# The second weight block waits for x, and the memory's norm moves back by one to two ticks

## The chip, the cores and the metric

The kernel runs on one core of a Trainium2 chip. The core has four compute engines with a stream of instructions each: the matrix engine TensorE (PE in the rows, PEld for its weight loads), VectorE (DVE), ScalarE (ACT) and GpSimd (POOL). SyncE (SP) computes nothing here, it issues transfers. Each engine takes its own instructions strictly in order; between engines only semaphores order the work. The metric is the device time of one execution in microseconds (us).

## The reference

Two layers over 256 tokens of width 1024, batch 1, all in 32-bit floats. Each layer adds three things to x in turn: a mixing part, a cross-attention to 256 memory rows, and an expert part that gathers 16 of 16,384 experts for each of 8 heads. Cut to its core:

```python
for l in range(DEPTH):
    h = rmsnorm(x, norm_mix_g[l])
    p_conv, p_attn, p_ssm = split(h @ w_in[l])          # u, val, gate, q, k, v
    y_conv, y_attn, y_ssm = conformer_conv(p_conv), stick_breaking_attention(p_attn), s5_ssm(p_ssm)
    x = x + concat(rmsnorm(y_conv), rmsnorm(y_attn), rmsnorm(y_ssm)) @ w_out[l]
    x = x + memory_cross_attention(rmsnorm(x, norm_mem_g[l]), rmsnorm(mem, mem_norm_g[l]),
                                   w_mq[l], w_mkv[l], w_mo[l])
    x = x + peer_ffn(rmsnorm(x, norm_ffn_g[l]), peer_wq[l], peer_sub_keys[l], peer_u[l], peer_v[l])
return rmsnorm(x, final_norm_g)
```

The change concerns the first microseconds of layer 0: `h @ w_in` for the first 128 tokens, and `rmsnorm(mem, mem_norm_g[0])` with the first products of it, the memory's keys `mem_h @ w_mkv`.

## The kernel before

The 256 tokens are two chunks of 128, and with two layers there are four stages, numbered ci = 0 to 3. In each stage the chunk's normed rows are transposed to `hT` (8 tiles of 128 x 128), multiplied by weight blocks, and worked through convolution, state space model, attention, memory attention and expert queries. A weight block is 1 MB (1024 rows by 256 columns, as `[128, 2048]`). The blocks are named by what they make: u, val, gate, q (two), k (two), v (two), mk (four, the memory's keys), mv (four), and more. Each gives 16 matmuls of 128 x 128 per chunk, which the trace lists as 32 records. The expert part of a stage makes 128 gathers, each of which brings one expert's row of 8 KB for every token of the chunk (1 MB; 512 gathers in all, the first at about 178 us), while the next stage's blocks run between them.

The program is written by a schedule of ticks. Every engine has a list of generators ("strands"), one for each piece of work of a stage. A strand yields the tick at which its next piece is due; the writer of an engine goes through the ticks, and at each tick through the strands in the order of the list, and puts down all that is due. So the tick numbers and the list's order fix the order of instructions on each engine. They fix nothing between engines; that is done by semaphores alone.

Around the change stage 0 stands so:

- **SP** (`block.sync`) issues x (first 128 rows), the small parameters `prm` (68 KB), the gain rows, and then the blocks in the order in which PE takes them (`issue`, one number j for each). Some other transfers are put ahead of a certain j: the memory's rows (`memX`, 1 MB) ahead of j = 2, the parameter matrices (768 KB) ahead of j = 3, the other 128 rows of x ahead of j = 5. The first blocks need no free buffer, so nothing holds them.
- **DVE** runs the set-up of the state space model's phases (`setup`, small operations one after another, each waiting for the one before), and between them the memory's norm (`mem_norm`, L1643 to L1655): two sums of squares of 128 x 1024 when the memory is in (L1649), and later a reciprocal of the roots (L1655).
- **ACT** (`mem_keys` there, from L1381) takes the root (L1390), scales the first 128 memory rows (L1395, semaphore `mem_scaled`), copies PE's transposes of them out of PSUM with the gain (L1404, eight copies), then does the same for the second 128 rows.
- **PE** (`mem_keys` there, from L914) transposes each 128 memory rows by 8 matmuls into the banks 4 and 7 (L924) once `mem_scaled` is there; the second set needs the same two banks emptied by ACT's copies. With both sets copied it multiplies by mk and mv (L946, L949). The products with `hT` (L467 for blocks up to k, `mix_lins`) come in between.

The ticks of PE for the blocks are in `MIX_AT`: u 6 and 7, val 8 and 9, gate 10 and 11, q0 12 and 13, q1 15 and 16. In one tick `mix_lins` comes ahead of `mem_keys`, on ACT too. `KEYS_AT` holds the ticks of the 32 pieces of mk and mv.

Of the kernel before, what the change touches and what calls it, by code (L numbers as in the profile page):

```python
# [75 lines left out]
BEGIN = [0] + [G0 + PER * i + 4 for i in range(NST - 1)]  # L76
# [8 lines left out]
def att_tick(ci, g, step):  # L85
# [2 lines left out]

KEYS_AT = [[15, 15] + [13 + i * 27 // 18 for i in range(2, 14)] + [32, 32, 34, 35, 37, 38] + [40 + i for i in range(8)]
           + [53 + i for i in range(4)],
           [113 + i * 3 // 4 for i in range(32)]]

# [67 lines left out]
def build(nc, x_d, mem_d, blocks_d, prm_d, rows_d, experts_d, out_d):  # L162
    ctx = ExitStack()
    with ctx:
# [141 lines left out]
        x_in = [sem(f"x_in{c}") for c in range(NC)]  # L306
# [121 lines left out]
        def _(eng):  # L428
# [484 lines left out]

            def mem_keys(l):  # L914
                at = BEGIN[l]
                tick = [11, 13] if l == 0 else [101, 104]
                for m in range(2):
                    yield at + tick[m]
                    eng.wait_ge(mem_scaled, 2 * l + m + 1)
                    for i in range(2):  # L920
                        fill((4, 7)[i], ("mem x", m, i, l))
                        for a in range(4):
                            k = 4 * i + a
                            last = nc.tensor.transpose(bank[(4, 7)[i]][:, a * P:(a + 1) * P],  # L924
                                                       memX[l][:, m, k * P:(k + 1) * P], ident[:, :])
                        last.then_inc(filled[(4, 7)[i]], 1)
                n = 0
                for kind in ("mk", "mv"):
                    for i in range(4):
                        for q in range(4):  # L930
                            yield at + KEYS_AT[l][n]
                            if n == 0:
                                for m in range(2):
                                    for a in range(2):
                                        read_out(("mem x", m, a, l))
                            n += 1
                            if q == 0:
                                b = i % 2 if l == 0 else (7, 4)[i % 2]
                                fill(b, (kind, i, l))
                                w, j = take(NC * l, FIRST[kind] + i)  # L940
                                w = w.rearrange("p (k n) -> p k n", k=KT)
                                free_with(j, b)
                            a = q // 2
                            for k in range(4 * (q % 2), 4 * (q % 2) + 4):
                                if kind == "mk":
                                    last = mm(bank[b][:, a * M:(a + 1) * M], w[:, k, a * P:(a + 1) * P],  # L946
                                              memH[l][:, k, :], start=k == 0, stop=k == KT - 1)
                                else:
                                    last = mm(bank[b][:, a * BW:(a + 1) * BW], memH[l][:, k, a * P:(a + 1) * P],  # L949
                                              w[:, k, :], start=k == 0, stop=k == KT - 1)  # L950
                        last.then_inc(filled[b], 1)
# [28 lines left out]
        def _(eng):  # L980
# [13 lines left out]
            for j in range(len(order)):  # L994
                if spots[j][0] >= POCKET:
                    l, p = order[j][0], spots[j][0]
# [6 lines left out]
            for j in issue:  # L1003
                l, n = order[j]
                what = LIN[n]
                if what == "u" and j:
                    stage += 1
                    if stage == 2:
                        full(("gain", 1, 1))
                        nc.sync.dma_start(gains[:, :], rows_d[1, :, :]).then_inc(rows_in, 16)  # L1010
                        full(("keys", HEADS[1][-1], 1))
                        nc.sync.dma_start(keys[:, :, :].rearrange("p t n -> p (t n)"),
                                          blocks_d[NBLK + NLIN, :, :]).then_inc(keys_in, 16)
                if j == 2:
                    nc.sync.dma_start(memX[0][:, :, :], mem_d.rearrange("(m p) d -> p m d", p=P))\
                        .then_inc(mem_in, 16)
                if j == 3:
                    nc.sync.dma_start(prm[:, NVEC:], prm_d[0, :, NVEC:]).then_inc(mats_in, 16)
                if j == 5:
                    nc.sync.dma_start(x[:, 1, :], x_d[P:S, :]).then_inc(x_in[1], 16)  # L1020
                if n == FIRST["mo"] and stage == 0:
                    nc.sync.dma_start(keys[:, :, :].rearrange("p t n -> p (t n)"), blocks_d[NLIN, :, :])\
                        .then_inc(keys_in, 16)
                if n == FIRST["mq"] + 2 and stage == 1:
                    read_out(("mem norm", 1, 1))
                    nc.sync.dma_start(prm[:, 0:NVEC], prm_d[1, :, 0:NVEC]).then_inc(prm_in, 16)
                    nc.sync.dma_start(prm[:, NVEC:], prm_d[1, :, NVEC:]).then_inc(mats_in, 16)
                if n == FIRST["wq"] + 2 and stage == 1:
                    full(("mo", 1, 1))
                    nc.sync.dma_start(memX[1][:, :, :], mem_d.rearrange("(m p) d -> p m d", p=P))\  # L1030
                        .then_inc(mem_in, 16)
                p, _ = spots[j]
                if lain(j) is not None:
                    done, count = free_at[lain(j)]
                    eng.wait_ge(done, count)
                if p == WIDE + STAY:
                    full(("mem t", 1, 0))
                if p == WIDE + STAY + 1:
                    full(("mo", 1, 0))
                if p == POCKET:  # L1040
                    full(("att o", 1, NC * l + 1))
                if p == POCKET + 1:
                    full(("ssm y", NC * l + 1))
                nc.sync.dma_start(home(p), blocks_d[l * NBLK + n, :, :]).then_inc(loaded[p], 16)
# [50 lines left out]
        def _(eng):  # L1095
# [284 lines left out]

            def mem_keys(l):  # L1381
                at = BEGIN[l]
                yield at + (9 if l == 0 else 98)
                if l == 0:
                    eng.wait_ge(mem_squared, 2)
                else:
# [2 lines left out]
                        step(act(squaresM, memX[l][:, m, :], ACT.Square, accum_out=mss[:, m:m + 1]))  # L1389
                act(mroot[:, :], mss[:, :], ACT.Sqrt, scale=1.0 / D, bias=epsb[:, :]).then_inc(mem_root, 1)  # L1390
                for m in range(2):
                    yield at + ((10, 11) if l == 0 else (100, 103))[m]
                    if m == 0:
                        eng.wait_ge(mem_rs, l + 1)
                    act(memX[l][:, m, :], memX[l][:, m, :], ACT.Copy, scale=mrs[:, m:m + 1]).then_inc(mem_scaled, 1)  # L1395
                    for i in range(2):
                        yield at + ((12, 14) if l == 0 else (102, 105))[m]
                        name = ("mem x", m, i, l)
                        src = full(name)
                        if m == 0 and i == 0:  # L1400
# [92 lines left out]
        def _(eng):  # L1493
# [149 lines left out]
            def mem_norm(l):  # L1643
                if l == 0:

                    yield BEGIN[l] + 8
                    eng.wait_ge(mem_in, 16)
                    for m in range(2):
                        v.tensor_tensor_reduce(out=htok[:, 0, :], in0=memX[0][:, m, :], in1=memX[0][:, m, :],  # L1649
                                               scale=1.0, scalar=0.0, op0=ALU.mult, op1=ALU.add,  # L1650
                                               accum_out=mss[:, m:m + 1]).then_inc(mem_squared, 1)
                        eng.wait_ge(mem_squared, m + 1)
                yield BEGIN[l] + (9 if l == 0 else 99)
                eng.wait_ge(mem_root, l + 1)
                v.reciprocal(mrs[:, :], mroot[:, :]).then_inc(mem_rs, 1)  # L1655

# [366 lines left out]
            for tick in range(LAST):  # L2023
                n = tick - G0
                ph, m = divmod(n - PER - 2, PER)
# [105 lines left out]
```

## Time and profile before

| what | value |
|---|---|
| device time, median of 3 runs | 1704.11 us (1704.04 to 1705.34) |
| the profiled execution | 1705.58 us |
| its span, first to last instruction | 1703.6 us |
| mean granted clock of TensorE | 0.991 |
| busy: PE / DVE / ACT / POOL | 91% / 71% / 36% / 34% |
| bytes moved | 675.16 MB, mean 396 GB/s |
| share of the chain that ended last: PE / transfers / DVE | 37% / 32% / 11% |

A busy share is a mean over the whole span, and stages differ: the table tells which engines are loaded, and the stretches below tell where. In a row of an engine's order of time the first number is the start in us from the span's start, the second the duration of the whole group, then engine, line of the kernel, operation, `written <- read` by the names of the program, and how many records; the bracket is the idle time just ahead of it and what ended it. The memory's buffers lie in `slots`, as the early weight blocks do, so `slots` stands for both; the line tells which.

### The profile page before, as it was taken

The page shows a single profiled execution, that of the slowest core. Times are in us where ns is not written, and L with a number is a line of the kernel's source. Part 1 is how long each engine was busy: PE and PEld are TensorE (multiplying, and loading weights), DVE is VectorE, ACT ScalarE, POOL GpSimd, SP SyncE. Part 2 cuts the span into 40 slices and gives each one's busy share as a digit, 9 for nine tenths or more (in the row PEclk, how much of TensorE's full clock was granted, in tenths as well). Part 3 has the DMA queues.
Part 4 walks back from the last instruction along what each step waited for, and adds up shares of the span by engine and source line. Part 5 has one row for each costly group of instructions (what it writes and reads, how often), then busy time and mean ns, then how long its engine had stood idle before and what let it go on. Part 6 is the DMA issues. An engine that isn't in the chain of part 4 may idle for free.

```text
span 1703.6 us, 19646 instructions
## 1 busy us (share of the span) xinstructions
PE 1556.9 (91%) x6618; PEld 941.8 (55%) x6618; DVE 1214.9 (71%) x3361; ACT 606.3 (36%) x1459; POOL 581.6 (34%) x527
## 2 busy tenths in 40 slices
PE   9999999899999999989999889988999998777776
PEld 8877776446567776544645446544656554232332
DVE  7821899985887659987555678986666777667665
ACT  4142433653354223364322242364333323222222
POOL 0000344442334323344333342343333544343431
PEclk9999999999999999999999999999999999999999
DMA  9655999999999999999999999999999999999996
GB/s 384 254 197 201 373 415 421 418 418 421 421 420 409 420 414 420 420 420 419 421 421 421 421 415 420 386 386 414 421 415 412 421 421 422 421 421 422 421 421 265
DMA packets 93860, 675.16 MB, mean 396 GB/s; under 512 B 10408, under 2 KB 10688, under 8 KB 12224
## 3 DMA queue, kind: packets, MB, share of 16 engines
q0 software_dynamic: 73728, 536.90, 76.3%
q1 hardware_dynamic: 20032, 137.00, 19.9%
q8 instruction: 53, 0.87, 0.2%
q14 instruction: 47, 0.39, 0.1%
HBM read 672.81 MB, written 1.05 MB: 396 GB/s over the span
## 4 chain that ended last, share of the span: by engine, by line
PE 37%; DMA 32%; DVE 11%; ACT 4%; issue 2%; POOL 0%; DVEq 0%; POOLq 0%
DMA slots<-expert_rows,expert 32%; PE bank L961 20%; PE bank L467 7%; DVE slots L1962 4%; PE bank L650 3%; PE bank L949 2%; PE bank L946 2%; ACT diag L1461 1%; DVE sg L1500 1%; DVE htok L1777 1%; ACT L1474 1%; DVE coef L1500 1%; PE bank L738 1%; DVE x L1500 0%; PE bank L475 0%
## 5 line engine op out<-in xcount | busy, mean ns | idle before, releaser
L961 PE MATMUL bank<-slots,diag 128*128 128x512 f32 x1916 | 903.6, 608 | 127.2 <-ACT diag L1461 123.8
L1089 POOL DMA_INDIRECT slots<-expert_rows,expert x512 | 579.6, 1132 | 1097.0 <-PE bank L961 868.7
L1962 DVE CUSTOM_DVE_ANT_0 slots<-slots,htok 128x1024 f32<-128x1024 f32 x512 | 625.7, 1223 | 276.5 <-DMA slots<-expert_rows,expert 275.2
L961 PEld LDWEIGHTS bank<-slots,diag 128*128 128x128 f32 x1916 | 347.1, 192 | 536.7 <-issue 318.6
L1474 ACT ACTIVATE gel<-dot 128x2 f32<-128x2 f32 (+1 forms) x258 | 52.5, 203 | 603.2 <-DVE dot L1962 602.4
L1461 ACT ACTIVATE diag<-ident,coef 128x128 f32<-128x128 f32 x479 | 168.3, 394 | 200.3 <-DVE coef L1500 197.2
L467 PEld LDWEIGHTS bank<-hT,ring 128*128 128x128 f32 x1488 | 179.5, 192 | 40.2 <-issue 37.8
L467 PE MATMUL bank<-hT,ring 128*128 128x128 f32 x1488 | 180.6, 275 | 1.8 <-DMA ring<-w_blocks 0.9
L1500 DVE SCALAR_TENSOR_TENSOR coef<-gel,ginv,gexp 128x2 f32<-128x2 f32 (+1 forms) x258 | 55.0, 213 | 83.2 <-ACT gel L1474 81.7
L1474 ACT ACT_TABLE_LOAD x67 | 86.0, 1283 | 1.2
L1500 DVE SCALAR_TENSOR_TENSOR sg<-pad,prm,sg 128x128 f32<-128x128 f32 x240 | 71.7, 344 | 0.0
L650 PE MATMUL bank<-ring,hT 128*128 128x512 f32 x104 | 48.2, 592 | 0.0
L650 PE MATMUL bank<-ring,products 128*128 128x512 f32 x96 | 45.1, 592 | 0.0
L1962 DVE DVE_READ_ACCUMULATOR2_ANT dot<- 128x1 f32 x512 | 42.3, 83 | 0.0
L1500 DVE SCALAR_TENSOR_TENSOR x<-slots,coef,x 128x1024 f32<-128x1024 f32 x33 | 42.2, 1280 | 0.0
L467 PEld LDWEIGHTS bank<-hT,slots 128*128 128x128 f32 x352 | 40.9, 192 | 2.0 <-issue 1.8
L467 PE MATMUL bank<-hT,slots 128*128 128x128 f32 x352 | 41.5, 275 | 0.2 <-DMA slots<-w_blocks 0.2
L467 PEld LDWEIGHTS bank<-hT,kept 128*128 128x128 f32 x256 | 31.7, 197 | 6.3 <-issue 6.3
L650 PEld LDWEIGHTS bank<-ring,hT 128*128 128x128 f32 x104 | 19.5, 190 | 23.4 <-issue 23.4
L1437 ACT ACT_TABLE_LOAD x25 | 32.1, 1283 | 0.4
L467 PE MATMUL bank<-hT,kept 128*128 128x128 f32 x256 | 31.8, 280 | 0.0
L650 PEld LDWEIGHTS bank<-ring,products 128*128 128x128 f32 x96 | 18.0, 190 | 21.5 <-issue 21.5
(350 smaller groups left out, 1563.1 us busy)
## 6 DMA issues: line engine op xcount, KB each, us to landing
ring<-w_blocks SPq DMA_DIRECT2D x90, 1024.0 KB, 9.3
slots<-w_blocks SPq DMA_DIRECT2D x24, 1024.0 KB, 11.4
slots<-expert_rows,expert POOLq DMA_INDIRECT x512, 15.4
kept<-w_blocks SPq DMA_DIRECT2D x4, 1024.0 KB, 12.4
keys<-w_blocks SPq DMA_DIRECT2D x2, 1024.0 KB, 11.1
kv<-w_blocks SPq DMA_DIRECT2D x2, 1024.0 KB, 13.4
prm<-small SPq DMA_DIRECT2D x2, 768.0 KB, 13.5
x<-x_rows SPq DMA_DIRECT2D x2, 512.0 KB, 11.1
```

What stands on the lines that cost most here:

```text
L467: last = mm(bank[b][:, a * P:(a + 1) * P], w[:, k, a * P:(a + 1) * P], src[:, k, :], start=k == 0, stop=k == KT - 1)
L650: last = mm(bank[b + i][:, :], src[:, first + k, :], w[:, k, i * 512:(i + 1) * 512], start=start and k == 0, stop=stop and k == 1)
L738: last = mm(bank[4][:, (2 * h + i) * P:(2 * h + i + 1) * P], memV[:, m, hh * MD + i * P:hh * MD + (i + 1) * P], mPT[:, hh, m, :], start=m ...
L946: last = mm(bank[b][:, a * M:(a + 1) * M], w[:, k, a * P:(a + 1) * P], memH[l][:, k, :], start=k == 0, stop=k == KT - 1)
L949: last = mm(bank[b][:, a * BW:(a + 1) * BW], memH[l][:, k, a * P:(a + 1) * P], w[:, k, :], start=k == 0, stop=k == KT - 1)
L961: last = mm(bank[h][:, :], diag[:, i % DIAGS, :], slots[:, SLOT[n], D + h * 512:D + (h + 1) * 512], start=m == 0, stop=n == end)
L1089: nc.gpsimd.indirect_dma_start(slots[:, s, :], None, experts_d, bass.IndirectOffsetOnAxis(ap=idx[q % 2][:, k:k + 1], axis=0),).then_inc(ar ...
L1437: act(gexp[:, j, :], best[:, j, :], ACT.Exp, bias=nbest[:, j, :], accum_out=gsum[:, j, :])\
L1461: act(diag[:, i % DIAGS, :], ident[:, :], ACT.Copy, scale=coef[:, q % 2, k:k + 1])\
L1474: act(gel[:, q % 2, k:k + many], dot[:, q % 2, k:k + many], ACT.Gelu_apprx_tanh).then_inc(gelu_ready, 1)
L1500: return v.scalar_tensor_tensor(out=out, in0=in0, scalar=scalar, in1=in1, op0=op0, op1=op1)
L1962: v.tensor_tensor_reduce(out=slots[:, s, 0:D], in0=slots[:, s, 0:D], in1=htok[:, ph % 2, :], scale=1.0, scalar=0.0, op0=ALU.mult, op1=ALU.add,
```

## The change

Three things are altered, all in stage 0. SP waits for x before it issues the second block (j = 1), and what was put ahead of j = 2 and j = 3 goes ahead of j = 3 and j = 4: the memory's rows behind the third block, the parameter matrices behind the fourth. On DVE and ACT the pieces of the memory's norm are due two ticks later, the last copies one. On PE the first transposes are due at 13 instead of 11, the second at 14 instead of 13, and the first two pieces of mk at 16 instead of 15.

```diff
-KEYS_AT = [[15, 15] + [13 + i * 27 // 18 for i in range(2, 14)] + ...
+KEYS_AT = [[16, 16] + [13 + i * 27 // 18 for i in range(2, 14)] + ...
 # PE, mem_keys
-                tick = [11, 13] if l == 0 else [101, 104]
+                tick = [13, 14] if l == 0 else [101, 104]
 # SP
-                if j == 2:
+                if j == 1:
+                    eng.wait_ge(x_in[0], 16)
+                if j == 3:
                     nc.sync.dma_start(memX[0][:, :, :], ...).then_inc(mem_in, 16)
-                if j == 3:
+                if j == 4:
                     nc.sync.dma_start(prm[:, NVEC:], prm_d[0, :, NVEC:]).then_inc(mats_in, 16)
 # ACT, mem_keys
-                yield at + (9 if l == 0 else 98)
+                yield at + (11 if l == 0 else 98)
-                    yield at + ((10, 11) if l == 0 else (100, 103))[m]
+                    yield at + ((12, 13) if l == 0 else (100, 103))[m]
-                        yield at + ((12, 14) if l == 0 else (102, 105))[m]
+                        yield at + ((14, 15) if l == 0 else (102, 105))[m]
 # DVE, mem_norm
-                    yield BEGIN[l] + 8
+                    yield BEGIN[l] + 10
-                yield BEGIN[l] + (9 if l == 0 else 99)
+                yield BEGIN[l] + (11 if l == 0 else 99)
```

PE's order in the opening, from the blocks u and val (`hT,ring`) over gate and q0 (`hT,slots`) to q1 and the first drive matmuls (L530); L924 are the memory's transposes:

```order
 L467 MATMUL bank<-hT,ring 128x128 x32
-L467 MATMUL bank<-hT,slots 128x128 x16
-L924 MATMUL bank<-ident,slots 128x128 x8
-L467 MATMUL bank<-hT,slots 128x128 x16
-L924 MATMUL bank<-ident,slots 128x128 x8
+L467 MATMUL bank<-hT,slots 128x128 x32
+L924 MATMUL bank<-ident,slots 128x128 x16
 L467 MATMUL bank<-hT,slots 128x128 x8
 L530 MATMUL bank<-uT,prm 128x128 x8
```

The two sets of transposes, which had q0 between them, now stand together behind q0.

ACT's order from the copy of u to the last copies of the memory, before. `mroot` is the root, L1395 the two scalings, L1404 the two sets of copies; `va`, `sg` and `qT` are the copies of val, gate and q0:

```order
L1156 ACTIVATE uT<-bank 128x256
L1390 ACTIVATE mroot<-mss,epsb 128x2
L1158 ACTIVATE va<-bank 128x256
L1395 ACTIVATE slots<-slots,mrs 128x1024
L1160 ACT_TABLE_LOAD
L1160 ACTIVATE sg<-bank 128x256
L1404 ACTIVATE slots<-bank,prm 128x128 x8
L1395 ACTIVATE slots<-slots,mrs 128x1024
L1163 ACTIVATE qT<-bank 128x256
L1404 ACTIVATE slots<-bank,prm 128x128 x8
```

And in the changed kernel, whose lines are numbered two higher from here on:

```order
L1158 ACTIVATE uT<-bank 128x256
L1160 ACTIVATE va<-bank 128x256
L1392 ACTIVATE mroot<-mss,epsb 128x2
L1162 ACT_TABLE_LOAD
L1162 ACTIVATE sg<-bank 128x256
L1397 ACTIVATE slots<-slots,mrs 128x1024
L1165 ACTIVATE qT<-bank 128x256
L1406 ACTIVATE slots<-bank,prm 128x128 x8
L1397 ACTIVATE slots<-slots,mrs 128x1024
L1406 ACTIVATE slots<-bank,prm 128x128 x8
```

The first scaling went from ahead of gate's sigmoid to behind it, and q0's copy from between the second scaling and its copies to ahead of the first copies. On both sides the second scaling stands behind the first eight copies.

DVE's order around the memory's squares (`htok,mss`) and the reciprocal, before, from the end of the first square on:

```order
L1649 ISA mss 128x1
L1649 ISA htok,mss<-slots 128x1024
L1649 ISA mss 128x1
L1500 SCALAR_TENSOR_TENSOR ssm_small<-ssm_small,powi 128x8
L1547 TENSOR_TENSOR ssm_small<-ssm_small 128x8
L1548 TENSOR_SCALAR ssm_small<-ssm_small 128x8
L1549 TENSOR_SCALAR ssm_small<-ssm_small 128x8
L1500 SCALAR_TENSOR_TENSOR ssm_small<-ssm_small 128x8 x3
L1552 TENSOR_SCALAR ssm_small<-ssm_small 128x8
L1553 TENSOR_SCALAR ssm_small<-ssm_small 128x8
L1500 SCALAR_TENSOR_TENSOR ssm_small<-ssm_small 128x8
L1655 RECIPROCAL mrs<-mroot 128x2
```

And in the changed kernel, from just ahead of the squares:

```order
L1558 TENSOR_SCALAR ssm_small<-ssm_small 128x8
L1562 TENSOR_SCALAR w<-times,ssm_small 128x129 x7
L1651 ISA htok,mss<-slots 128x1024
L1651 ISA mss 128x1
L1651 ISA htok,mss<-slots 128x1024
L1651 ISA mss 128x1
L1562 TENSOR_SCALAR w<-times,ssm_small 128x129
L1563 TENSOR_SCALAR w<-w 128x1032
L1502 SCALAR_TENSOR_TENSOR w<-times,ssm_small,w 128x129 x8
L1657 RECIPROCAL mrs<-mroot 128x2
```

The squares moved behind 20 set-up operations, seven of them on 129 columns (`w<-times`). Between the squares and the reciprocal stand ten operations on both sides: small ones of 8 columns before, now one of 129 columns, one of 1032 and eight of 129.

## Rows read from the trace of the kernel before

**Rows 1.** The page: busy time of each engine, and GB/s in 40 slices.
```profile
PE 1556.9 (91%) x6618; PEld 941.8 (55%) x6618; DVE 1214.9 (71%) x3361; ACT 606.3 (36%) x1459; POOL 581.6 (34%) x527
...
GB/s 384 254 197 201 373 415 421 418 418 421 421 420 409 420 414 420 420 420 419 421 421 421 421 415 420 386 386 414 421 415 412 421 421 422 421 421 422 421 421 265
```

**Rows 2.** Busy time by stretch: us, each engine, PEclk, DMA share, GB/s.
```profile
26.40:131.00 104.60, 104.58 (x582) 84.71 (x580) 62.78 (x182) 33.53 (x75) 0.00 (x0) 1.00 0.63 249
131.00:193.00 62.00, 56.30 (x377) 46.31 (x378) 23.24 (x91) 20.30 (x50) 7.01 (x7) 1.00 0.69 258
193.00:197.50 4.50, 4.50 (x16) 3.01 (x15) 2.70 (x7) 0.00 (x0) 0.93 (x1) 0.62 1.01 424
```

**Rows 3.** PE's order of time, 9.65 to 28 us: start, duration, group, wait before.
```profile
9.65 7.38 PE L467 MATMUL bank<-hT,ring 128*128 128x128 f32 x64 [0.93 <-DMA ring<-w_blocks]
17.23 3.81 PE L467 MATMUL bank<-hT,slots 128*128 128x128 f32 x32 [0.20 <-DMA slots<-w_blocks]
20.88 1.04 PE L924 MATMUL bank<-ident,slots 128*128 128x128 f32 x8
21.75 3.74 PE L467 MATMUL bank<-hT,slots 128*128 128x128 f32 x32
25.50 1.09 PE L924 MATMUL bank<-ident,slots 128*128 128x128 f32 x8
26.43 1.95 PE L467 MATMUL bank<-hT,slots 128*128 128x128 f32 x16
```

**Rows 4.** SP's order of time: the issues of the first two blocks.
```profile
2.07 0.82 SPq L1044 DMA_DIRECT2D ring<-w_blocks  x2
```

**Rows 5.** ACT's order of time, x, hT and the memory's norm.
```profile
4.45 1.06 ACT L1119 ACTIVATE hT<-x 128x1024 f32<-128x1024 f32 x1 [1.56 <-DMA x<-x_rows]
...
7.94 2.18 ACT L1125 ACTIVATE hT<-bank,prm 128x128 f32<-128x128 f32 x8 [1.38 <-PE bank L475]
...
19.50 1.15 ACT L1395 ACTIVATE slots<-slots,mrs 128x1024 f32<-128x1024 f32 x1 [1.66 <-DVE mrs L1655]
...
22.24 2.17 ACT L1404 ACTIVATE slots<-bank,prm 128x128 f32<-128x128 f32 x8
24.24 1.20 ACT L1395 ACTIVATE slots<-slots,mrs 128x1024 f32<-128x1024 f32 x1
...
26.19 2.18 ACT L1404 ACTIVATE slots<-bank,prm 128x128 f32<-128x128 f32 x8 [0.28 <-PE bank L924]
```

**Rows 6.** DVE's order of time, 11.9 to 29.5 us.
```profile
11.94 0.17 DVE L1534 TENSOR_SCALAR powi<-ssm_small 128x8 int32<-128x8 f32 x1
14.74 1.22 DVE L1649 CUSTOM_DVE_ANT_0 htok<-slots 128x1024 f32<-128x1024 f32 x1 [2.63 <-DMA slots<-mem_rows]
...
17.27 0.17 DVE L1500 SCALAR_TENSOR_TENSOR ssm_small<-ssm_small,powi 128x8 f32<-128x8 f32 x1
...
19.30 0.17 DVE L1655 RECIPROCAL mrs<-mroot 128x2 f32<-128x2 f32 x1
...
19.97 2.55 DVE L1560 TENSOR_SCALAR w<-times,ssm_small 128x129 f32<-128x129 f32 x8
22.55 0.70 DVE L1561 TENSOR_SCALAR w<-w 128x1032 f32<-128x1032 f32 x1
23.29 6.19 DVE L1500 SCALAR_TENSOR_TENSOR w<-times,ssm_small,w 128x129 f32<-128x129 f32 x16
```

**Rows 7.** PE's order of time behind three long waits.
```profile
192.69 2.78 PE L961 MATMUL bank<-slots,diag 128*128 128x512 f32 x4 [3.08 <-ACT diag L1461]
195.26 2.86 PE L467 MATMUL bank<-hT,kept 128*128 128x128 f32 x16
...
335.46 1.98 PE L961 MATMUL bank<-slots,diag 128*128 128x512 f32 x4 [2.34 <-ACT diag L1461]
...
791.55 3.42 PE L961 MATMUL bank<-slots,diag 128*128 128x512 f32 x4 [2.87 <-ACT diag L1461]
```

**Rows 8.** DVE's order of time: the first step of the routing.
```profile
172.70 0.30 DVE L1895 MAX8 tops<-bank 128x8 f32<-128x128 f32 x1 [1.62 <-PE bank L805]
```

More of the change, by code:

```diff
@@ L87, in att_tick @@
     return BEGIN[ci] + 31 + 4 * g + step if ci else (30, 31, 32, 32, 33, 34, 35, 36)[step] + 3 * g
-KEYS_AT = [[15, 15] + [13 + i * 27 // 18 for i in range(2, 14)] + [32, 32, 34, 35, 37, 38] + [40 + i for i in range(8)]
+KEYS_AT = [[16, 16] + [13 + i * 27 // 18 for i in range(2, 14)] + [32, 32, 34, 35, 37, 38] + [40 + i for i in range(8)]
            + [53 + i for i in range(4)],
```

## The prediction

> **What bounds the kernel now.** I read the page's totals first, then the busy shares by stretch, then each engine's order of time in the opening. The totals show the matrix engine busy for 1556.9 of 1703.6 us, and the line of GB/s at about 420 in nearly all slices from the fifth on [rows 1]: the long middle, where 512 expert gathers run, is bound by transfers. The change touches only the opening, up to about 190 us, where the stretches show another bound: from 26.4 to 131 us the matrix engine (PE) is busy 104.58 of 104.60 us, with the transfers at 249 GB/s [rows 2]. An in-order engine without idle time hands on every delay that it gets. From 131 to 193 us it idles 5.7 us (62.00 less 56.30) [rows 2]. Before 26.4 us its order of time has two small waits, 0.93 us for the first weight block u and 0.20 us for the third [rows 3].
>
> So the question is what the change does to PE up to its first matmul on the fifth block (q1), which starts at 26.43 us [rows 3] with the work of four blocks and of the memory's 16 transposes behind it. It needs the same work there afterwards.
>
> **The change part by part.** *The second block waits for x.* The queue issues u and the second block from 2.07 us on [rows 4]. x is in at 4.45 us, when ScalarE (ACT) starts on it [rows 5], so the second block is issued about 2 us later, and all that stands behind it on SP (third block, memory, fourth block, the parameter matrices, the rest) moves with it. What is queued by then, x, 68 KB and u, is still under way, since u is used only at 9.65 us [rows 3]. Does u come sooner? It has at most the 0.93 us wait to give, and the third block's wait adds 0.20 us: a gain between nothing and 1.1 us. I take 0.4, because the vector hT that the same matmuls need is not whole before 7.94 + 2.18 = 10.12 us [rows 5], by which time PE is only about half a microsecond into the block. This gain does not reach the sum, as follows.
>
> The Trainium skill (DMA: Bandwidth & Descriptors, "Queues, rings and completion order") says that each transfer engine takes the descriptors of one queue in ring order. By that u is already ahead of the second block on every engine and gains nothing. The trace has no row that decides it: u and the second block were never apart. By the rule the sum below is the same, and by a gain of the whole wait it is the same too.
>
> *The memory's rows behind the third block.* The memory's squares start at 14.74 us as its rows land, and PE takes up the third block at 17.23 us [rows 6, 3]: one block of 1 MB is worth 17.23 - 14.74 = 2.5 us of landing. So the memory should start at about 14.74 + 2.5 = 17.24 us. The bounds: 14.74 us if u's relief pulls all forward, and 2 us more than 17.24 if the whole delay of the issue is passed on.
>
> *The norm's pieces.* VectorE (DVE) no longer stalls 2.63 us before the squares. From 12.11 us (11.94 + 0.17) it first does what stood between 17.27 and the last of the eight L1560 operations, 19.97 + 7 x 0.32 = 22.2, less 0.08 for the reciprocal: 4.9 us, so it is ready at 17.0 [rows 6]. The squares then start at 17.24 (or 17.0 if the memory is early) and take 17.27 - 14.74 = 2.53, to 19.77. Behind them the new order puts one more L1560 (0.32), L1561 (0.74 to the next start) and eight of the sixteen L1500 (8 x 0.39 = 3.1) ahead of the reciprocal, which therefore starts at 23.95 and not at 19.30 [rows 6]. ACT starts the first scaling 0.2 later, as from 19.30 to 19.50 [rows 6, 5], and takes 1.15: PE gets the first half of the memory at about 25.35. The old chain had it at 20.65, just before PE asked at 20.88.
>
> PE now does four blocks in a row first. Even without the gain at the start they end at 9.65 + 7.38 + 3.7 + 3.74 = 24.4 us, with it at 24.0. So PE waits 1.0 to 1.35 us for the first half, whichever it is: an earlier u only lengthens the wait, and this is why u is not in the sum.
>
> *The two sets of transposes stand side by side.* Before, the matmuls of q0 (3.74 us) ran between them and covered ACT. In the new order nothing does. From the start of the first set ACT needs 0.69 us until the first bank is full (25.50 to 26.19), 2.00 for the eight copies (22.24 to 24.24), and 1.20 for the second scaling [rows 5, 3]: with 0.1 for the signal PE may start the second set 4.0 us after the first. Its own first set takes 0.93 (25.50 to 26.43) [rows 3]. PE idles about 3.05 us. q0's 3.74 us of cover is gone, and no instruction may be taken from behind in its place. The result: first set 25.35, second 29.35, q1 at 30.25. That is 30.25 - 26.43 = 3.8 us late.
>
> *The clock.* After the gap of 3.08 us the granted clock was 0.62 in the mean of the next 4.5 us, so partly at 1.2 instead of 2.4 GHz [rows 2]; the next matmuls took 2.78 and 2.86 us [rows 7], where such groups take 1.98 [rows 7] and 1.95 [rows 3]: 1.7 us lost. After a gap of 2.87 us four took 3.42, 1.44 more; after 2.34 us they took 1.98 [rows 7]. A gap of 3.05 lies with the first two, so I add 1.6 us; the ends are nothing and 1.7.
>
> The Trainium skill (TensorE: Matmul & The Clock Gate, "HAM oscillation — how this bites in real kernels") says that waits between bursts leave the array cold again, and that the price is paid once for each. That rule speaks against this change twice, at the wait of about 1.2 us and at that of 3.05. Rows 7 agree for gaps of 2.9 us and up, not for the one of 2.34. By the rule alone the sum would hold a second 1.6 us.
>
> **The sum.** 3.8 + 1.6 = 5.4 us late at q1. The gap-free PE carries it to 131 us. Behind that the first routing step waits for PE's scores, 1.62 us before 172.70 [rows 8], so the gathers start as much later; and since the transfers then run at a constant rate and move the same bytes, the end moves too. The profiled execution took 1705.58 us (span 1703.6 and 1.98 around it), which is 1.47 above the median of the runs. Against its own time I get 1711.0; against the median 1704.11 + 5.4 = **1709.5 us**.
>
> **The rivals.** *Only the wait, without the clock* (or the clock's fall lies in the idle time): 3.8 us, 1707.9. For it: a gap of 2.34 us had no fall. Against it: both gaps next to 3 us had one. *The memory is later*, because the restarted queue runs dry: up to 2 us on top of 5.4, since everything from the squares to the second set follows the landing one for one; 1711.5. Against it: u is still moving when the second block is issued. *Two falls of the clock*, by the second rule: 5.4 + 1.6, 1711.1. *Not slower: the lateness is swallowed* at PE's later waits. They hold 5.7 us up to 193 us [rows 2], a little more than the 5.4. It decides if what they wait for is not itself late; then the end is 1704 to 1706. Against it: those waits are for ACT and DVE, which are working on PE's own results [rows 8]. *Faster*: the lot runs as intended and PE never waits on the memory. Its ceiling is the 1.1 us of the two small waits, 1703.0, and it needs the 4.0 us between the two sets not to be there. *The change doesn't do what it says*: u lands as before. Then PE waits 1.0 and not 1.35, and the end is the same 1709.5.
>
> **How the numbers follow.** 0.2% is 3.4 us, about what a measurement of this kernel can tell from no change, so slower begins at 1707.5 and faster ends at 1700.7. Chances: the forecast, with u early or not, 0.50; without the clock 0.20 (some of it below 1707.5); memory later 0.10; two falls 0.05; swallowed in good part 0.12; faster or nearly so 0.03. Faster by over 0.2% has no mechanism in these rows beyond scatter: 0.03. Same: most of the 0.12, a third of the 0.20 and the ceiling case, 0.22. Slower 0.75. The likeliest case's own range, with clock and landing at their bounds, is 1707.7 to 1711.0. The range for eight in ten reaches down into the swallowed case and up to the late memory: 1705.5 to 1711.5.
>
> **What would show it.** Right: PE idle about 1 us before the first set of transposes (named after ACT), then about 3 us between the two sets; the reciprocal of the memory's norm near 24 us; q1 about 3.8 us later; the matmuls behind the gap at 1.2 GHz for a while; the first gather 5 us later than before. The step on the transposes is wrong if the two sets stand less than 2 us apart, and the step on the reciprocal if PE waits for nothing ahead of the first. The step on passing on is wrong if q1 is 5 us late and the first gather is not. A landing of u clearly before 9.5 us would show that the second block disturbed it.

## The result, and the profile after

| | before | after |
|---|---|---|
| device time, median of 6 runs each | 1704.18 us (1704.04 to 1705.79) | 1710.72 us (1710.10 to 1713.67) |
| ratio after / before, 95% interval | | 1.0037 (1.0027 to 1.0047) |
| profiled execution (span) | 1705.58 us (1703.6) | 1710.52 us (1708.5) |

The change makes the kernel 6.5 us slower. The forecast was 1709.5, with a range of 1705.5 to 1711.5 and a chance of 0.75 for slower.

PE's order of time in the opening of the kernel after shows where it went; it answers to [rows 3]. L467 are the products with `hT`: u and val in the first row, gate and q0 in the second, q1 at 31.12; L924 are the two sets of transposes; the last row is k0, the block that follows q1 and the first products of the memory's keys:

```profile
9.80 7.38 PE L467 MATMUL bank<-hT,ring 128*128 128x128 f32 x64 [0.76 <-DMA ring<-w_blocks]
17.02 7.31 PE L467 MATMUL bank<-hT,slots 128*128 128x128 f32 x64
25.40 1.09 PE L924 MATMUL bank<-ident,slots 128*128 128x128 f32 x8 [1.07 <-ACT slots L1397]
29.36 1.97 PE L924 MATMUL bank<-ident,slots 128*128 128x128 f32 x8 [2.87 <-ACT slots L1397]
31.12 3.62 PE L467 MATMUL bank<-hT,slots 128*128 128x128 f32 x16
34.67 1.19 PE L530 MATMUL bank<-uT,prm 32*128 32x128 f32 x16
...
44.58 3.73 PE L467 MATMUL bank<-hT,slots 128*128 128x128 f32 x32
```

The same k0 in the kernel before, with the same work ahead of it:

```profile
38.19 3.73 PE L467 MATMUL bank<-hT,slots 128*128 128x128 f32 x32
```

k0 starts 44.58 - 38.19 = 6.39 us later. The brackets give four of its parts: u starts 0.15 later (9.80 for 9.65), the third block's wait of 0.20 is gone, PE waits 1.07 ahead of the first transposes and 2.87 between the two sets. That is 3.89 us of start and waiting. The rest, 2.50, is in durations: the second set takes 1.97 (the first 1.09), and the first half of q1 3.62, where [rows 3] have 1.95. The stretches of the kernel after say why. The columns are those of [rows 2]; look at the eighth item, the granted clock:

```profile
28.00:34.70 6.70, 5.34 (x26) 5.12 (x26) 6.30 (x12) 5.47 (x13) 0.00 (x0) 0.50 1.01 421
26.40:131.00 104.60, 101.72 (x549) 82.29 (x549) 60.82 (x176) 34.65 (x77) 0.00 (x0) 0.97 0.61 240
```

From 28 to 34.7 us the grant is 0.50 of full speed: 1.2 instead of 2.4 GHz, from the second gap until the end of q1's first half; the second half, at 35.79, takes 2.05 again. The second row answers to the first of [rows 2]: PE, which had no idle time there, now has 104.60 - 101.72 = 2.9 us of it, the gap.

DVE's order of time, the squares (L1651), the eight L1502 and the reciprocal (L1657), answers to [rows 6]:

```profile
17.30 1.23 DVE L1651 CUSTOM_DVE_ANT_0 htok<-slots 128x1024 f32<-128x1024 f32 x1 [0.44 <-DMA slots<-mem_rows]
...
20.89 3.08 DVE L1502 SCALAR_TENSOR_TENSOR w<-times,ssm_small,w 128x129 f32<-128x129 f32 x8
24.00 0.17 DVE L1657 RECIPROCAL mrs<-mroot 128x2 f32<-128x2 f32 x1
```

The squares wait 0.44 for the memory and start at 17.30; the reciprocal comes at 24.00. ACT's order of time, the two scalings (L1397) and the eight copies (L1406) between them, answers to [rows 5]:

```profile
24.20 1.15 ACT L1397 ACTIVATE slots<-slots,mrs 128x1024 f32<-128x1024 f32 x1 [2.37 <-DVE mrs L1657]
...
26.09 2.18 ACT L1406 ACTIVATE slots<-bank,prm 128x128 f32<-128x128 f32 x8 [0.48 <-PE bank L924]
28.11 1.20 ACT L1397 ACTIVATE slots<-slots,mrs 128x1024 f32<-128x1024 f32 x1
```

ACT idles 2.37 us until the reciprocal, scales at 24.20, copies at 26.09 and scales the second half from 28.11 to 29.31; PE starts the second set at 29.36. So the 3.96 us from set to set are ACT's chain, as computed.

SP's issues answer to [rows 4]:

```profile
2.07 2.56 SPq L1046 DMA_DIRECT2D ring<-w_blocks  x2
...
5.27 0.66 SPq L1017 DMA_DIRECT2D slots<-mem_rows  x1
```

Both first blocks stand in one row of 2.56 us, which holds the wait for x; the memory is issued at 5.27.

The delay reaches the end of the opening unchanged. DVE's first routing step answers to [rows 8], and behind it stands the first gather on POOL, of the kernel after and then of the kernel before:

```profile
179.09 0.30 DVE L1897 MAX8 tops<-bank 128x8 f32<-128x128 f32 x1 [1.62 <-PE bank L805]
```

```profile
184.79 1.09 POOL L1091 DMA_INDIRECT slots<-expert_rows,expert  x1 [182.14 <-DVE expert L1502]
```

```profile
178.41 1.09 POOL L1089 DMA_INDIRECT slots<-expert_rows,expert  x1 [175.76 <-DVE expert L1500]
```

The routing is 179.09 - 172.70 = 6.39 us late, the first gather 6.38, the median end 6.5. PE's busy time rises from 1556.9 [rows 1] to 1559.2 us, by 2.3. The slow stretch, the same matmuls at half clock, is 2.5 of lengthening; the rest is not accounted for, as the clock falls at other places too, and not at the same ones in both executions.

### The profile page after: what moved, and what is told of

It is laid out like the page before. It is cut to its first block, busy times and chain, and to the rows that moved or that the text cites. A ratio compares the mean times of both kernels' runs of the same rounds, so it can differ in the third digit from the quotient of the medians.

```text
span 1708.5 us, 19646 instructions
## 1 busy us (share of the span) xinstructions
PE 1559.2 (91%) x6618; PEld 945.4 (55%) x6618; DVE 1213.3 (71%) x3361; ACT 606.1 (35%) x1459; POOL 581.0 (34%) x527
## 4 chain that ended last, share of the span: by engine, by line
PE 36%; DMA 30%; DVE 14%; ACT 4%; issue 2%; POOL 0%; DVEq 0%; POOLq 0%
DMA slots<-expert_rows,expert 30%; PE bank L961 19%; PE bank L467 7%; DVE slots L1964 6%; PE bank L650 3%; PE bank L949 2%; PE bank L946 2%; DVE sg L1502 1%; ACT diag L1463 1%; DVE htok L1779 1%; DVE coef L1502 1%; ACT L1476 1%; PE bank L738 1%; DVE products L1708 0%; DVE x L1502 0%
## 5 line engine op out<-in xcount | busy, mean ns | idle before, releaser
L467 PEld LDWEIGHTS bank<-hT,ring 128*128 128x128 f32 x1488 | 179.5, 192 | 40.0 <-issue 37.8
L467 PE MATMUL bank<-hT,ring 128*128 128x128 f32 x1488 | 180.6, 275 | 1.6 <-ACT hT L1127 0.8
L1502 DVE SCALAR_TENSOR_TENSOR coef<-gel,ginv,gexp 128x2 f32<-128x2 f32 (+1 forms) x258 | 54.7, 212 | 93.5 <-ACT gel L1476 91.7
L1502 DVE SCALAR_TENSOR_TENSOR sg<-pad,prm,sg 128x128 f32<-128x128 f32 x240 | 71.3, 341 | 0.0
L467 PEld LDWEIGHTS bank<-hT,slots 128*128 128x128 f32 x352 | 43.3, 202 | 1.7 <-issue 1.4
L467 PE MATMUL bank<-hT,slots 128*128 128x128 f32 x352 | 44.0, 286 | 0.0
L1502 DVE SCALAR_TENSOR_TENSOR x<-slots,coef,x 128x1024 f32<-128x1024 f32 x33 | 42.2, 1279 | 0.0
L467 PEld LDWEIGHTS bank<-hT,kept 128*128 128x128 f32 x256 | 30.6, 192 | 5.7 <-issue 5.7
L467 PE MATMUL bank<-hT,kept 128*128 128x128 f32 x256 | 30.8, 275 | 0.0
```

Of the source, the lines that this page charges most:

```text
L467: last = mm(bank[b][:, a * P:(a + 1) * P], w[:, k, a * P:(a + 1) * P], src[:, k, :], start=k == 0, stop=k == KT - 1)
L1502: return v.scalar_tensor_tensor(out=out, in0=in0, scalar=scalar, in1=in1, op0=op0, op1=op1)
```

## The experiments

Theory: the two sets of transposes side by side cost PE about 3 us of waiting, and the clock falls behind it. Rivals: the transfers cost the time; two waits cost two falls; the wait costs nothing but itself; the lateness is swallowed later on. The kernel before was run beside them, in two groups: 1704.72 us (for the first four kernels) and 1704.65 us. A matmul of zeros, where added, is extra work whose product nobody reads. "Late" below is the first gather against 178.41.

| kernel | median, us (runs) | ratio, 95% interval | first gather, late by |
|---|---|---|---|
| changed kernel | 1710.72 (6) | 1.0037 (1.0027 to 1.0047) | 6.38 |
| ticks alone | 1711.50 (5) | 1.0039 (1.0025 to 1.0053) | 5.24 |
| transfers alone | 1707.45 (11) | 1.0018 (1.0009 to 1.0027) | 3.50 |
| changed, gap filled | 1709.32 (8) | 1.0027 (1.0016 to 1.0037) | 3.50 |
| before, busy delay | 1709.10 (8) | 1.0024 (1.0014 to 1.0035) | 4.45 |
| changed, second set behind q1 | 1705.86 (11) | 1.0006 (0.9997 to 1.0015) | 0.58 |
| that, and reciprocal at once | 1703.96 (11) | 0.9998 (0.9989 to 1.0007) | -0.28 |
| before, second block waits | 1704.62 (11) | 1.0001 (0.9992 to 1.0010) | -0.15 |
| changed, second block waits for u | 1712.09 (1) | not timed | 6.92 |

Single executions of one kernel lie mostly within 2 us, and up to 3.4 us, from its median, so the gather of the profiled execution is the finer measure, and the medians only bear it out.

**Ticks alone.** The changed kernel with the transfers issued as before:

```diff
-                if j == 1:
-                    eng.wait_ge(x_in[0], 16)
-                if j == 3:
+                if j == 2:
...
-                if j == 4:
+                if j == 3:
```

> The changed kernel with its transfers issued as before: the second block does not wait for x, the memory's rows stand ahead of the third block. Only the ticks of the memory's norm are new. Theory (the lost time is the order on DVE, ACT and PE): the memory lands at 14.6 us again, but DVE reaches the squares only at 17.0, so nothing is won: PE waits about 0.9 us ahead of the first transposes and 2.9 us between the two sets, the clock falls, the first gather is about 6 us later than before, and the time is about 1710.4 us. Rival (the later transfers cost it): the time of the kernel before, 1704.2 us.

PE's order of time, u and val, q0, the two sets, q1:

```profile
10.36 7.38 PE L467 MATMUL bank<-hT,ring 128*128 128x128 f32 x64 [1.65 <-DMA ring<-w_blocks]
...
23.20 3.81 PE L467 MATMUL bank<-hT,slots 128*128 128x128 f32 x32 [1.48 <-DMA slots<-w_blocks]
26.85 1.04 PE L924 MATMUL bank<-ident,slots 128*128 128x128 f32 x8
30.75 1.09 PE L924 MATMUL bank<-ident,slots 128*128 128x128 f32 x8 [2.86 <-ACT slots L1395]
31.68 1.95 PE L467 MATMUL bank<-hT,slots 128*128 128x128 f32 x16
```

The stretch behind the gap:

```profile
30.00:36.00 6.00, 5.25 (x52) 5.01 (x53) 4.15 (x9) 5.22 (x12) 0.00 (x0) 1.00 1.02 423
```

The gap of 2.86 us is there with the memory early: the order alone makes it. The 1.48 ahead of q0 I had not expected, and the new ticks do not explain it: PE asks for q0's block at 21.72 (23.20 - 1.48), no sooner than the 21.75 at which it had it in the kernel before [rows 3], and the transfers are issued in the old order. u is 0.71 late as well (10.36 for 9.65). So up to 2.2 of the 5.24 us are transfers that came late in this execution; why stays open. The first set then waits for nothing, where 0.9 was expected. And the clock did not fall: 1.00 from 30 us on, and the second set takes 1.09. A gap of 2.86 us therefore need not cost a fall, which was expected to come. The five executions lie in two groups, 1708.89 and 1709.29 (the traced one) and 1711.50 to 1712.06. The 2.2 to 3.2 us between them are about what a fall costs below, but the upper three have no trace, so that they had one is not shown.

**Transfers alone.** The kernel before with the changed kernel's SP:

```diff
-                if j == 2:
+                if j == 1:
+                    eng.wait_ge(x_in[0], 16)
+                if j == 3:
...
-                if j == 3:
+                if j == 4:
```

> The kernel before with only the transfers changed: the second block waits for x, the memory's rows stand behind the third block, the parameter matrices behind the fourth; the ticks are as before. Theory: the memory is in at 17.2 us, DVE stalls ahead of the squares until then (5.1 us instead of 2.6), the reciprocal comes at 21.8, PE waits about 2.5 us ahead of the first transposes (23.2 us) and some 0.3 ahead of the second; q1 is about 2.6 us late and, if the clock falls after a gap of 2.5 us, about 1.6 more: 1706.8 to 1708.4 us. Rival (the issue order helps u): PE starts u before 9.3 us and the time is not above 1704.2 us.

PE's order of time, first set, q0, second set, q1; then the stretch of q0:

```profile
22.92 1.09 PE L924 MATMUL bank<-ident,slots 128*128 128x128 f32 x8 [2.46 <-ACT slots L1397]
23.85 5.37 PE L467 MATMUL bank<-hT,slots 128*128 128x128 f32 x32
29.05 1.04 PE L924 MATMUL bank<-ident,slots 128*128 128x128 f32 x8
29.93 1.95 PE L467 MATMUL bank<-hT,slots 128*128 128x128 f32 x16
```

```profile
23.80:29.00 5.20, 5.20 (x34) 5.20 (x33) 4.75 (x13) 3.85 (x11) 0.00 (x0) 0.67 1.01 416
```

In the old order the later memory makes PE wait 2.46 us ahead of the first set, and the clock falls: q0 takes 5.37, in the busy delay below 3.73. q1 is 29.93 - 26.43 = 3.50 late (2.6 expected, 4.2 with a fall), and so is the first gather; the 0.3 expected ahead of the second set did not come. Each half of the change costs time alone; the later ticks take away 1.4 of this wait (2.46 to 1.07) and add the gap of 2.87.

**The gap filled.** Three matmuls of zeros, 128x128 by 128x512, between the two sets of the changed kernel:

```diff
+                    if l == 0 and m == 0:
+                        for _ in range(3):
+                            mm(bank[0][:, :], cands[:, 0:P], cands[:, :], start=True, stop=True)
```

> The changed kernel with three more matmuls of zeros (128 x 512) on PE between the two sets of the memory's transposes, into a bank that is not used yet; their results are not read. They take about 2.6 us of the gap of 2.87. Theory (the loss is 3.8 us of waiting and the rest is the clock): the wait itself stays, the second set still starts at 29.4 us, but the granted clock stays at 1.0, q1 starts at about 30.3 and the first gather is about 3.9 us later than before instead of 6.4: about 1708.1 us. Rival (the clock costs nothing, everything is waiting): 1710.7 us as the changed kernel.

PE's order of time, first set, added matmuls (L929), second set, q1, k0:

```profile
25.05 1.09 PE L924 MATMUL bank<-ident,slots 128*128 128x128 f32 x8 [1.03 <-ACT slots L1400]
25.98 2.74 PE L929 MATMUL bank<-cands 128*128 128x512 f32 x6
29.01 1.09 PE L924 MATMUL bank<-ident,slots 128*128 128x128 f32 x8 [0.28 <-ACT slots L1400]
29.94 1.95 PE L467 MATMUL bank<-hT,slots 128*128 128x128 f32 x16
...
41.70 3.73 PE L467 MATMUL bank<-hT,slots 128*128 128x128 f32 x32
```

The spacing of the sets is the same 3.96, but PE is busy in it and the second set takes 1.09, q1's half 1.95. From the first set to k0 it is 41.70 - 25.05 = 16.65 us, in the changed kernel 44.58 - 25.40 = 19.18: in these two executions the clock's fall is worth 2.53 us, and keeping PE busy with nothing useful gives all of it back. The medians, 6.5 and 4.6 us above the kernel before, agree within their intervals. The gather came 3.50 late and not 3.9, since u started at 9.32 here and at 9.80 in the changed kernel.

**A busy delay.** Six such matmuls behind the first set of the kernel before, so that PE is late without a wait:

```diff
+                    if l == 0 and m == 0:
+                        for _ in range(6):
+                            mm(bank[0][:, :], cands[:, 0:P], cands[:, :], start=True, stop=True)
```

> The kernel before with six more matmuls of zeros (128 x 512) on PE behind the first set of the memory's transposes, 5.2 us of work that nobody reads; nothing else is changed. Theory (a delay of PE in the opening reaches the end whole): no gap and no fall of the clock near 30 us, q1 and the first gather 5.2 us later, and a time of about 1709.4 us. Rival (later waits swallow it): the first gather less than 2 us later, 1704.2 to 1706 us.

PE's order of time, added matmuls, q0, q1:

```profile
21.28 5.32 PE L929 MATMUL bank<-cands 128*128 128x512 f32 x12
26.43 3.73 PE L467 MATMUL bank<-hT,slots 128*128 128x128 f32 x32
...
30.87 1.95 PE L467 MATMUL bank<-hT,slots 128*128 128x128 f32 x16
```

q1 is 30.87 - 26.43 = 4.44 us late (5.15 from the added matmuls to q0, of which an earlier start gave 0.47 back and the absent wait ahead of gate 0.20). The first gather is 4.45 late and the median 4.4. What PE loses in the opening reaches the end, as far as the scatter lets one see; nothing shows that any of it is swallowed.

**The second set behind q1.** The changed kernel, with only PE's ticks of the second set and of the first keys moved:

```diff
-KEYS_AT = [[16, 16] + [13 + i * 27 // 18 for i in range(2, 14)] + ...
+KEYS_AT = [[19, 19] + [max(19, 13 + i * 27 // 18) for i in range(2, 14)] + ...
-                tick = [13, 14] if l == 0 else [101, 104]
+                tick = [13, 16] if l == 0 else [101, 104]
```

> The changed kernel with the second set of the memory's transposes moved behind the fifth block (q1) on PE, and the first pieces of the memory's keys behind the sixth. The 3 us of q1 and the first drive matmuls then lie in the gap of 2.87 us. Theory: the wait ahead of the first set stays (about 1 us), the one between the sets and the fall of the clock go; the first gather is about 1.1 us later than in the kernel before and the time 1.1 us above it, 1705.3 to 1705.8 us. Rival (the late memory norm itself costs, wherever the transposes stand): 4 to 6 us above the kernel before.

PE's order of time, first set, q1, second set, k0:

```profile
25.22 1.09 PE L924 MATMUL bank<-ident,slots 128*128 128x128 f32 x8 [0.99 <-ACT slots L1397]
26.15 1.95 PE L467 MATMUL bank<-hT,slots 128*128 128x128 f32 x16
...
31.01 1.04 PE L924 MATMUL bank<-ident,slots 128*128 128x128 f32 x8
31.88 3.74 PE L467 MATMUL bank<-hT,slots 128*128 128x128 f32 x32
```

The first set still waits 0.99, and then nothing waits: the gap is covered by q1, and the slow stretch is gone with it. The first gather is 0.58 late instead of 6.38, and the time cannot be told from before. So the adjacency of the two sets, and what it did to the clock, is 5.8 of the 6.38 us, or 5.6 without the 0.18 by which the first set starts earlier here (25.22 for 25.40).

**And the reciprocal at once.** The same, with the reciprocal one tick earlier, ahead of the eight L1502:

```diff
-                yield BEGIN[l] + (11 if l == 0 else 99)
+                yield BEGIN[l] + (10 if l == 0 else 99)
```

> As the run with the second set behind q1, and in addition the reciprocal of the memory's norm stands directly behind the squares on DVE (tick 10 instead of 11), ahead of the ten long operations. The memory then is scaled from about 21.9 us on, behind the gate's sigmoid. Theory: PE has no wait on the memory any more, q1 and the first gather stand within 0.5 us of the kernel before, and the time is that of the kernel before within 0.7 us. With that the whole loss is in the two waits and the clock. Rival (something else in the change costs): 2 us or more above the kernel before.

PE's order of time, u and val, first set, q1; then the reciprocal on DVE:

```profile
10.05 7.38 PE L467 MATMUL bank<-hT,ring 128*128 128x128 f32 x64 [1.04 <-DMA ring<-w_blocks]
...
24.41 1.04 PE L924 MATMUL bank<-ident,slots 128*128 128x128 f32 x8
25.29 1.95 PE L467 MATMUL bank<-hT,slots 128*128 128x128 f32 x16
```

```profile
20.55 0.17 DVE L1657 RECIPROCAL mrs<-mroot 128x2 f32<-128x2 f32 x1 [0.43 <-ACT mroot L1392]
```

The reciprocal at 20.55 (24.00) takes the wait ahead of the first set away, so that one came from the L1502 put in front of it. PE has no wait left behind 10.05 in the opening, yet the kernel is only as fast as before (0.9989 to 1.0007): u came 0.40 later in this execution and the first gather 0.28 earlier, so all that PE saved behind u is about 0.7 us. This run and the one before it keep the changed transfers: with this order on PE and DVE they cost nothing that shows, and the 3.50 of the transfers alone belong to them together with the old order.

**The second block's wait alone.** The kernel before with one wait more on SP:

```diff
+                if j == 1:
+                    eng.wait_ge(x_in[0], 16)
```

> The kernel before with one line more: the second block is issued when x is in; the memory's rows stay ahead of the third block, the ticks are as before. Theory (each transfer engine takes a queue's work in order, so u gains nothing): u lands between 8.8 and 10.2 us as in all the runs so far, the memory where it did, and the time is that of the kernel before within 0.7 us. Rival (the second block disturbs u): u lands before 8.5 us, PE starts u up to 0.5 us earlier; the time then is at most 0.5 us lower, which the times alone would not tell.

PE's order of time, u and val:

```profile
9.55 7.38 PE L467 MATMUL bank<-hT,ring 128*128 128x128 f32 x64 [0.79 <-DMA ring<-w_blocks]
```

PE starts u at 9.55 us, before 9.65 [rows 3]; time and first gather as before. Holding the second block back costs nothing that shows. It does not speed u up by more than the 0.1 us between two single executions, and u's start varies by more than that without it (9.65 and 10.36 in two kernels that do not hold the block back), so a gain of a few tenths is not excluded.

**The second block waits for u itself.** The changed kernel, so that nothing is queued behind u until it is in:

```diff
-                    eng.wait_ge(x_in[0], 16)
+                    eng.wait_ge(loaded[spots[0][0]], 16)
```

> The changed kernel with the second block waiting for u itself to land, so that nothing but x, the small parameters and the gain rows is under way beside u. A look at one landing. Theory (u's last parts are late by themselves): u lands between 8.8 and 10.2 us still. Rival (what is queued behind u slows it): u lands at 7 to 8 us. In both cases the second block comes late, PE waits for it, and the time is some us above that of the changed kernel.

PE's order of time, u, the second set, q1's first half, the first drive matmuls:

```profile
9.22 3.98 PE L467 MATMUL bank<-hT,ring 128*128 128x128 f32 x32 [0.41 <-ACT hT L1127]
...
31.12 1.97 PE L924 MATMUL bank<-ident,slots 128*128 128x128 f32 x8 [2.87 <-ACT slots L1397]
32.88 2.43 PE L467 MATMUL bank<-hT,slots 128*128 128x128 f32 x16
35.23 1.16 PE L530 MATMUL bank<-uT,prm 32*128 32x128 f32 x16
```

u starts at 9.22, and is not what PE waits for there (hT is). SP issues the second block at 8.73, and that is when u was in: just ahead of the 8.8 to 10.2 of the theory, and behind the 7 to 8 of the rival. hT came last in four others too, with u's start between 9.18 (busy delay, nothing held back) and 9.53 us, so u was in by then there as well, and one execution does not settle whether 8.73 is an effect or scatter. Issuing the blocks that late cost 0.49 us ahead of val and 1.13 ahead of q0. The clock again: after the same gap of 2.87 the second set takes 1.97, but q1's half 2.35 (32.88 to 35.23), so this fall cost 0.83 + 0.47 = 1.3 us, where the changed kernel lost 2.5.

## Why the prediction was right, step by step

- **The order decides.** Two transposes side by side, with ACT's fill, eight copies and scaling between them: 4.0 us predicted from start to start, 3.96 measured; the idle time 3.05 and 2.87 (the forecast counts the first set as 0.93, to the next start, the trace as 1.09). The starts, 25.35 and 29.35, came at 25.40 and 29.36. Undoing the adjacency takes away 5.6 to 5.8 of the 6.38 us. The step is shown.
- **The first wait.** 1.0 to 1.35 predicted, 1.07 measured. (The low end is 0.9 by the forecast's own terms: 9.65 + 7.38 + 3.7 + 3.74 is 24.47 and not 24.4.) The reciprocal was put at 23.95 and came at 24.00; with it moved forward the wait is gone, so the step on DVE's order is shown. The squares were put at 17.24 and came at 17.30: the memory is one block later, and the queue did not run dry.
- **u.** The 0.4 us of relief did not come; u is 0.15 later. As said, this is not in the sum. The Trainium skill (DMA: Bandwidth & Descriptors, "Queues, rings and completion order") says that each transfer engine takes the descriptors of a queue in ring order; from that the forecast argued that u gains nothing from the second block's delay. The start of 9.55 against 9.65 when that delay was made alone does not contradict it, but is too small a test to confirm it; with nothing queued behind u it was in at 8.73, once.
- **Passing on.** Predicted whole; 6.39 us at k0, 6.38 at the first gather, 6.5 at the median end (4.9 between the two profiled executions, within the scatter of single ones), and 4.44, 4.45 and 4.4 for the busy delay. The swallowed case, given 0.12, is out. (The upper end of the likeliest case's own range, 1711.0, does not come out of its bounds: 1704.11 + 3.8 + 1.7 + 2.0 is 1711.6. The stated range does not hang on it.)
- **The clock: the term that was too small.** 1.6 us predicted, 2.5 measured, which is what separates the sum of 5.4 from 6.4. I had read the price from two later gaps and taken it as the price of any gap. Here the grant is at half for the whole second set and the whole half of q1, 5.3 us of work at 0.50. That the fall came at all, as the forecast assumed, was in part luck: behind the same gap it did not come in the traced execution of the ticks alone.
- **Clock and gap.** The forecast put the fall down to the gap's length: yes at 2.9 us and up, no at 2.34. The runs contradict that: a fall after 2.46 (transfers alone), none after 2.86 (ticks alone), 2.5 and 1.3 us of loss after the same 2.87. What decided stays open. The changed kernel and the ticks alone differ in what went before the same gap: a wait of 1.07 us that ended at 25.40, or one of 1.48 that ended at 23.20. No run changes this alone. But where nine of the kernels have nearly the same wait behind the same matmuls, near 190 us, the clock fell in four and not in five (last section), so the gap and the work just ahead of it do not settle it.
- **One price for each wait?** The rule of the Trainium skill that I weighed (TensorE: Matmul & The Clock Gate, "HAM oscillation — how this bites in real kernels") would have added 1.6 for the wait of 1.07. The page tells it of waits for transfers that are longer than this one, so the forecast stretched it. Nor do the runs bear it out here: with the second gap filled or covered, the wait of 1.03 or 0.99 left the next matmuls at their normal durations; whether it helped to bring on the fall at the second gap is part of what stays open. A wait of 1.39 us near 193 us in the run with the second block's wait alone did have a price: the four records behind it took 3.27 us, where such groups take 1.98 at full clock. That two falls would have come to 1711.1, close to the result, is a coincidence of size.

## What to carry over

When pieces of a chain that goes back and forth between two engines are moved, look at what stands between them on the engine that bounds: a block of independent work between two steps was the cover for the other engine's turn, and two neat rows side by side expose the whole turn. An idle gap on the matrix engine costs its length and, sometimes, half speed behind it; take the price as a range from nothing to more than its nearest neighbours in the trace show, and try filling or covering the gap. A wait that a change sets out to remove is worth at most its own length: the two in front of PE were 1.1 us in all, against the 4 us of waiting that the new order put on the path.

## What the runs showed of the hardware

The granted clock does not follow from a gap's length. In the places shown so far it fell after 2.46, 2.87 and 3.08 us and did not after 1.48, 2.34 and 2.86. Nor does it follow from the length and the work just ahead together. Near 190 us the same wait of PE (ahead of L837, for ACT's copy of the expert queries) stands behind the same matmuls in nine of the ten kernels, all but the kernel before. It lasts 1.78 to 1.97 us, and the clock fell after 1.84, 1.86, 1.95 and 1.95 and did not after 1.78, 1.80, 1.81, 1.94 and 1.97. First PE's order of time and the stretch in the changed kernel, where it fell; then PE's order of time in the run with the second block's wait alone, where the wait was longer and it did not:

```profile
193.91 0.71 PE L837 MATMUL bank<-keys,qT 128*128 128x128 f32 x4 [1.84 <-ACT qT L1352]
194.46 2.95 PE L467 MATMUL bank<-hT,slots 128*128 128x128 f32 x16
```

```profile
193.90:197.50 3.60, 3.50 (x20) 3.20 (x20) 3.50 (x12) 0.44 (x2) 0.00 (x0) 0.68 1.01 428
```

```profile
187.49 0.71 PE L837 MATMUL bank<-keys,qT 128*128 128x128 f32 x4 [1.97 <-ACT qT L1352]
188.04 1.95 PE L467 MATMUL bank<-hT,slots 128*128 128x128 f32 x16
```

Sixteen records take 2.95 us in the first, where they take 1.95 at full clock, at a mean grant of 0.68. As far as these single traces show, the program's order alone does not tell whether a fall comes, so a forecast should carry its price as a chance times a cost.

And the last parts of the first block come late by an amount that differs from one traced execution to the next: where PE's wait for u came last, it ended at 9.55, 9.80 and 10.05 us in three kernels that hold the second block back until x is in, and at 9.65 and 10.36 in two that do not.
